# Hybrid decoder trunk on one core: the order of the last input tiles, the place of the scan's norm, and the order of the channels where the input projection turns into the output projection

## The reference

```python
h = rms_norm(x, norm_g)
u = h @ w_in
c_q, c_kv, k_pe, g_mla, u_conv, g_conv, z, xbc, dt_raw = jnp.split(u, offs, axis=-1)
o_mla = mla_mixer(...) * jax.nn.silu(g_mla)                  # 768 features
o_conv = conformer_conv_mixer(u_conv, ...) * jax.nn.silu(g_conv)   # 512; ends in layer_norm, silu, @ w_pw
o_ssd = ssd_mixer(z, xbc, dt_raw, ...)                       # 768; rms_norm(y * silu(z), norm_g)
y = jnp.concatenate([o_mla, o_conv, o_ssd], axis=-1) @ w_out
return x + y
```

## Time and profile before

| | |
|---|---|
| time, median of 3 runs | 1558.3 us (1558.18 to 1559.57) |
| profiled execution, its own time | 1560.33 us |
| its span in the trace | 1558.5 us |
| TensorE busy | 98% of the span |
| VectorE busy | 65% |
| ScalarE busy | 44% |
| mean DMA rate | 101 GB/s |

### The profile page before, as it was taken

The page is one execution under the profiler, slowest core; times in us unless marked ns, Lnnn a source line. Parts: engine busy times, 40 slices in busy tenths (PEclk is TensorE's granted clock), DMA queues, the critical chain, the costliest instruction groups (busy, mean ns, idle before and its releaser), DMA issues.

```text
span 1558.5 us, 18374 instructions
## 1 busy us (share of the span) xinstructions
PE 1525.9 (98%) x7062; PEld 1222.7 (78%) x7062; DVE 1007.0 (65%) x1496; ACT 687.6 (44%) x1014; POOL 44.7 (3%) x86
## 2 busy tenths in 40 slices
PE   7999999999999999999999999999999999999997
PEld 6777777778888887888887777778878887878885
DVE  7534674889998777443455456758999977762221
ACT  6445553434456645121253555533444575451110
POOL 0000000000000000110000000000000000000110
PEclk9999999999999999999999999999999999999999
DMA  6322222222233223544432222222223333234441
GB/s 224 94 92 81 82 82 81 68 82 68 81 111 114 89 83 96 176 142 142 142 102 78 87 89 82 95 68 68 77 73 102 99 116 98 88 99 158 150 140 62
DMA packets 44423, 158.13 MB, mean 101 GB/s; under 512 B 5520, under 2 KB 5808, under 8 KB 44336
## 3 DMA queue, kind: packets, MB, share of 16 engines
q1 hardware_dynamic: 36720, 129.64, 25.6%
q0 software_dynamic: 6464, 23.12, 5.1%
q10 hardware_dynamic: 1152, 4.19, 0.7%
HBM read 148.50 MB, written 8.44 MB: 101 GB/s over the span
## 4 chain that ended last, share of the span: by engine, by line
PE 84%; DVE 9%; ACT 4%; issue 1%; DMA 1%; ACTq 0%; DVEq 0%; POOL 0%; POOLq 0%
PE acc L494 19%; PE acc L496 18%; PE acc L495 18%; PE S L499 5%; PE S L494 3%; PE S L496 3%; PE S L495 3%; PE T L496 3%; PE T L494 3%; PE T L495 3%; DVE wlo L1022 2%; ACT L742 1%; PE M L499 1%; PE O L499 1%; DVE hlo L1105 1%
## 5 line engine op out<-in xcount | busy, mean ns | idle before, releaser
L494 PE MATMUL acc<-hhi,whi 128*128 128x512 f32 (+1 forms) x1504 | 600.6, 399 | 14.0 <-DVE wlo L1022 13.4
L496 PE MATMUL acc<-hhi,wlo 128*128 128x512 f32 (+1 forms) x1504 | 588.2, 391 | 0.0
L495 PE MATMUL acc<-hlo,whi 128*128 128x512 f32 (+1 forms) x1504 | 587.4, 391 | 0.0
L1022 DVE TENSOR_TENSOR wlo<-stage,whi 128x1024 fp32r<-128x1024 f32 (+2 forms) x252 | 300.7, 1196 | 411.5 <-ACT whi L754 408.1
L754 ACT ACTIVATE whi<-stage 128x1024 fp32r<-128x1024 f32 (+2 forms) x252 | 260.2, 1036 | 503.7 <-PE acc L496 281.4
L494 PEld LDWEIGHTS acc<-hhi,whi 128*128 128x128 f32 (+1 forms) x1504 | 282.2, 188 | 79.1 <-DVE wlo L1022 15.1
L496 PEld LDWEIGHTS acc<-hhi,wlo 128*128 128x128 f32 (+1 forms) x1504 | 281.8, 187 | 62.2
L495 PEld LDWEIGHTS acc<-hlo,whi 128*128 128x128 f32 (+1 forms) x1504 | 282.3, 188 | 60.8 <-issue 2.9
L1077 DVE SCALAR_TENSOR_TENSOR cacc<-glu,pv,cacc 128x512 f32<-128x512 f32 x240 | 168.8, 747 | 4.3 <-DVE cols L1161 0.3
L742 ACT ACT_TABLE_LOAD x67 | 86.0, 1283 | 7.5 <-issue 5.2
L494 PE MATMUL S<-hhi,whi 128*128 128x512 f32 x192 | 75.2, 392 | 0.0
(11 more groups left out here) (231 smaller groups left out, 1554.2 us busy)
## 6 DMA issues: line engine op xcount, KB each, us to landing
stage<-weights SPq DMA_DIRECT2D x236, 512.0 KB, 3.4
y_features<-xg POOLq DMA_DIRECT2D x32, 256.0 KB, 4.2
acsb<-acs_rows POOLq DMA_DIRECT2D x16, 384.0 KB, 4.1
xg<-x_features ACTq DMA_DIRECT2D x8, 512.0 KB, 9.3
xr<-x_features POOLq DMA_DIRECT2D x16, 256.0 KB, 4.1
xr<-y_features POOLq DMA_DIRECT2D x16, 256.0 KB, 4.1
stage<-weights SPq DMA_DIRECT2D x8, 256.0 KB, 2.6
stage<-weights SPq DMA_DIRECT2D x4, 384.0 KB, 3.0
```

Of the source, the lines that this page charges most:

```text
L494: nc.tensor.matmul(out, a, c, start=start, stop=False)
L495: nc.tensor.matmul(out, a, d, start=False, stop=False)
L496: return nc.tensor.matmul(out, b, c, start=False, stop=stop)
L1022: nc.vector.tensor_tensor(wlo[u % RING][:, 0:w], stage[u % STAGE][:, 0:w], whi[u % RING][:, 0:w].bitcast(F32), ALU.subtract).then_inc(lo_d ...
```

## The change

It does three things.

1. The last ten input tiles stand in the order z0, z1, z2, gconv0, gconv1, z3, z4, z5, gconv2, gconv3. z5 is now tile 38 (half tiles 76 and 77), gconv2 and gconv3 are tiles 39 and 40.
2. The scan's norm leaves the turn. `ssd_sum` is a hook of half tile 78, behind pw 0: TensorE waits for `ssd_sq` and multiplies by ones into bank `T[1]`, ScalarE does Ln and Exp. `ssd_scale` is a hook of half tile 79, behind pw 1: VectorE scales channels 10 to 15.
3. At the turn the channels are split and multiplied in the order `TURN_ORDER`: 0 to 7, then 10 to 15, then 8 and 9. The `out2` quarters take k = 0 to 7 for both rows first, then 10 to 15 for both, then 8 and 9. What was left of the old step `ssd_sum` is the step `turn_end`, which splits 10 to 15, then 8 and 9, and waits for the third and fourth pointwise product only ahead of 8 and 9.

```diff
-    t += [("gconv", j, [(_OFF["gconv"] + P * j, P)]) for j in range(4)]
-    t += [("z", j, [(_OFF["z"] + P * j, P)]) for j in range(6)]
-    return t
+    gate = [("gconv", j, [(_OFF["gconv"] + P * j, P)]) for j in range(4)]
+    z = [("z", j, [(_OFF["z"] + P * j, P)]) for j in range(6)]
+    return t + z[0:3] + gate[0:2] + z[3:6] + gate[2:4]
...
+    put(78, "ssd_sum")
+    put(79, "ssd_scale")
...
-    s.append(("ssd_sum", (), []))
+    s.append(("turn_end", (), []))
...
-OUT2 = [(0, k) for k in range(10)] + [(1, k) for k in range(10)]
-OUT2 += [(f, k) for f in range(2) for k in range(10, KX)]
+TURN_ORDER = list(range(8)) + list(range(10, KX)) + [8, 9]
+OUT2 = [(f, k) for f in range(2) for k in TURN_ORDER[:8]]
+OUT2 += [(f, k) for f in range(2) for k in TURN_ORDER[8:14]]
+OUT2 += [(f, k) for f in range(2) for k in TURN_ORDER[14:]]
...
+                    elif name == "ssd_sum":
+                        pe.wait_ge(ssd_sq.sem, ssd_sq.at(layer, 1))
+                        pe.wait_ge(ssd_in.sem, ssd_in.at(layer, 8))
+                        total(ssd_sum, [sqz[:, :]], T[1])
                     elif name == "out2":
...
-                        if quarter == 1:
-                            pe.wait_ge(ssd_sq.sem, ssd_sq.at(layer, 1))
-                            pe.wait_ge(pw_taken.sem, pw_taken.at(layer, 4))
-                            total(ssd_sum, [sqz[:, :]], M)
                         for i in range(8):
                             f, k = OUT2[8 * quarter + i]
-                            pe.wait_ge(h_lo.sem, h_lo.at(layer, KX + k + 1))
+                            pe.wait_ge(h_lo.sem, h_lo.at(layer, KX + TURN_ORDER.index(k) + 1))
...
                     elif name == "ssd_sum":
+                        act.wait_ge(ssd_sum.sem, ssd_sum.at(layer, 1))
+                        rsqrt(ssd_r, rcq[:, :], T[1][:, :], SSD_WIDTH, 0)
+                    elif name == "turn_end":
 
                         act.wait_ge(unit_used.sem, unit_used.at(layer, TILE_UNIT[len(TILES) - 1] + 1))
-                        act.wait_ge(pw_taken.sem, pw_taken.at(layer, 4))
-                        for k in range(8, KX):
-                            if k == 10:
-                                act.wait_ge(ssd_sum.sem, ssd_sum.at(layer, 1))
-                                rsqrt(ssd_r, rcq[:, :], M[:, :], SSD_WIDTH, 0)
+                        for k in TURN_ORDER[8:]:
                             if k >= 10:
                                 act.wait_ge(branch_ready.sem, branch_ready.at(layer, k - 9))
+                            else:
+                                act.wait_ge(pw_taken.sem, pw_taken.at(layer, k - 5))
                             branch_hi(k)
...
                     elif name == "turn":
-                        split_branch(0, 8)
-                    elif name == "ssd_sum":
-                        split_branch(8, 10)
+                        split_branch(TURN_ORDER[:8], 0)
+                    elif name == "ssd_scale":
                         dve.wait_ge(ssd_r.sem, ssd_r.at(layer, 1))
                         for k in range(10, KX):
                             stt(branch_ready, xg[:, k, :], xg[:, k, :], par("sng", k - 10), rcq[:, :], ALU.mult,
                                 ALU.mult, go=k < KX - 1)
-                            if k >= 12:
-                                split_branch(k - 2, k - 1)
-                        split_branch(KX - 2, KX)
+                    elif name == "turn_end":
+                        split_branch(TURN_ORDER[8:], 8)
```

More of the change, by code:

```diff
@@ L710, in _ @@
                             pe.wait_ge(acc_taken.sem, acc_taken.at(layer, len(TILES) - 1 + quarter))
-                        if quarter == 1:
-                            pe.wait_ge(ssd_sq.sem, ssd_sq.at(layer, 1))
-                            pe.wait_ge(pw_taken.sem, pw_taken.at(layer, 4))
-                            total(ssd_sum, [sqz[:, :]], M)
                         for i in range(8):
                             f, k = OUT2[8 * quarter + i]
-                            pe.wait_ge(h_lo.sem, h_lo.at(layer, KX + k + 1))
+                            pe.wait_ge(h_lo.sem, h_lo.at(layer, KX + TURN_ORDER.index(k) + 1))
                             last = three(out_bank(f)[:, :], *w(u, i * P, P), hhi[:, k, :], hlo[:, k, :],
-                                         k == 0, k == KX - 1)
+                                         k == 0, k == TURN_ORDER[-1])
                         last.then_inc(unit_used.sem, 1)
@@ L1099, in _, with split_branch @@
                         x_lo(k, 0)
-                def split_branch(first, end):
-                    for k in range(first, end):
-                        dve.wait_ge(h_hi.sem, h_hi.at(layer, KX + k + 1))
+                def split_branch(ks, before):
+                    for i, k in enumerate(ks):
+                        dve.wait_ge(h_hi.sem, h_hi.at(layer, KX + before + i + 1))
                         nc.vector.tensor_tensor(hlo[:, k, :], xg[:, k, :], hhi[:, k, :].bitcast(F32),
```

## The result

The changed kernel takes 1563.8 us (median of 12 runs, 1562.2 to 1565.1), the kernel before 1558.4 us (12 runs, 1558.0 to 1561.6). The ratio is 1.0027 with an interval of 1.0018 to 1.0035: slower by 0.27%, 4.2 us. The time lies in the range of the prediction, on the side of its rival B, and not at its point of 1559.8. The profiled execution took 1562.68 us around a span of 1560.9.

A forecast was written before the change was run, and what follows sets the result against it. TensorE, busy 98% of the span, bounds the kernel, so only its waits count. A layer loses 4.47 us at half tile 78 and regains 3.69 at the turn: +1.6 us in two, 1559.8 us from 1558.3; range 1557.0 to 1565.0.

The forecast's parts named there:

- rival B: In the stand at half tile 78 the clock falls: 2.4 us a fall, 1562.2 or 1564.6 us; chance 0.20.
- The wait at 78: Behind half tile 78 and pw0 TensorE waits for z5's last add; half tile 79 comes 4.47 us later.
- The turn: Both TensorE waits at the turn go: 3.69 us a layer back, 0.87 us of it only the ones-matmul moved.
- Rival D: At the turn waits of the old size stay, the scaling having delayed the eight splits: 1565.4 us; chance 0.08.
- The sum without the clock: A layer: +4.47 us at half tile 78 less 3.69 us at the turn, +0.78 us.
- the hitch inside quarter 2: A 0.1 us loss inside quarter 2 of `out2` at the turn, named only as an allowance in the range.
- The tiles, ScalarE and the scaling: Half tiles 62 to 67, norm table loads and 4.1 us of scaling passes stay hidden, costing the path nothing.
- A: TensorE's wait moves from the turn to half tile 78: 1559.8 us, called same; chance 0.64.
- The price of a fall: Behind the stand at half tile 78, twelve matmuls at 0.2 us more each: 2.4 us a fall.
- Rival C: At half tile 78 TensorE stands under 1.6 us, so the turn's gain decides: 1551.7 us, faster; chance 0.08.

The follow-up runs named there:

- e5: The changed kernel with one number changed: the hook `ssd_sum` at half tile 79 in place of 78, the scaling still at 79; 1553.7 us, ratio 0.9966.
- e7: The changed kernel with `ln_apply` 1 at half tile 77 in place of 76, behind z5's passes on VectorE; 1564.4 us, ratio 1.0031.
- e1: The changed kernel with four extra ones-matmuls, result overwritten, in TensorE's stand at half tile 78; 1562.15 us, ratio 1.0009.
- e11: The changed kernel with the attention stand filled and four extra ones-matmuls in the stand at half tile 78; 1559.2 us, ratio 0.9998.
- e8: The kernel before with two extra ones-matmuls ahead of the first transposition of probabilities, in attention; 1558.24 us, ratio 0.9994.
- e6: The changed kernel with one extra ones-matmul, result overwritten, in the stand at half tile 78; 1562.4 us, ratio 1.0018.
- e10: The changed kernel with the attention stand filled by extra ones-matmuls, nothing added at half tile 78; 1562.6 us, ratio 1.0018.
- e4: The kernel before with one wait added: behind half tile 78 and pw0 TensorE waits for z3's last add; 1570.9 us, ratio 1.0065.

## Why the prediction was right and where not

**The wait at 78** was right in place, cause and size: behind pw0, for the last add of z5, in VectorE's order behind `ln_apply`. TensorE stood 3.7 us by the profile's count, and the norm's matmul started 0.05 us behind the end of the add, not 0.15. e5 and e7 show the cause: one half tile later there is no stand, and with VectorE's order turned the stand moves to pw0.

**The turn** gave back what was forecast. No wait is left there; the scaling ends at 598.83, 1.8 us before the eight splits begin; the last quarter's weights are split in time. Rival D is out.

**The sum without the clock** was +0.78 us a layer and measured +0.53 (e1, e11). The term is over by 0.25 us: 0.1 is the shorter way from the add to the matmul, about 0.1 the hitch inside quarter 2 that also went, which I had named and not counted; the rest isn't resolved.

**The tiles, ScalarE and the scaling** cost nothing, as forecast. VectorE's idle time ahead of the split of half tile 68 shrank from 2.72 us to 0.67 us, by three passes, and the split itself, at 511.28 with the 1.89 us added, starts at the old 513.17:

```profile
511.28 1.23 DVE L1027 TENSOR_TENSOR wlo<-stage,whi 128x1024 fp32r<-128x1024 f32 x1 [0.67 <-ACT whi L758]
```

The additional table load for gconv2 is there at 589.59, under pw1 (588.66 to 591.47 on TensorE).

**The step that failed is the weight between A and B.** The likeliest case was a stand that costs its length, 1559.8 us, called the same; what happened is B, the fall in both layers, which had 0.20. The prediction said that the trace couldn't decide, since the spacing stayed 0.23 us behind the longest stands of the turn. That read too few rows. The windows of the granted clock in the kernel before show a fall at 240 to 246, behind a stand of 1.56 us, less than half as long as the one forecast. The like stand of layer 1 had none, so the trace made a fall possible and not certain; but a stand over twice as long should have had more than 0.20. The price of a fall was over: 2.4 us forecast, as twelve matmuls at half rate from the start of the kernel, 1.6 measured (55.92 less 54.30). The half clock lasted only 3.4 us here, and about 1.0 us of the price lay in the norm's own matmul and the product behind it, the rest in the next four. B's own sum, 1564.6, is high by 0.8 us of the median, the two errors of size going one way (-0.25 and -0.8 a layer), and the falls in attention, which come on top in most runs, the other. That it came so near is in part luck.

**Rival C** is out: there was no short wait.

In time without falls the change would cost 1.0 us (e11 against e8: runs of 1558.8 to 1559.7 against 1557.9 to 1558.9), under the 3.1 us that the prediction needed to tell a change from none. The measured 4.2 us are those 1.0 and two falls of 1.6. The stand itself was no small matter: e5, which has neither stand nor fall at 78, is 5.1 us a layer under the changed kernel, 3.5 more than the fall.

## What to carry to other kernels

When a join is moved earlier on TensorE, look up when its last input is made in the order of the engine that makes it; one half tile was the difference between 0.27% lost and 0.34% won. Where TensorE must stand between dense matmuls, count the fall of the clock behind the stand as well as the stand: here 1.6 us for most, 2.6 to 2.9 for some, behind stands of 1.6 to 4.3 us. Matmuls with a discarded result took the fall away where they filled nearly the whole stand (four in e1 and e11, 0.3 us of stand left); one of them was not enough (e6, 2.9 us left). And read the windows of the granted clock of the kernel before, since a fall that is already there warns of what a new stand may do.

## What the runs showed of the hardware

The clock fell behind a stand of only 1.56 us in some executions of the same program (e8 against the kernel before), and in one layer of the profiled execution and not the other. It fell at a stand of 2.9 us in both layers of the profiled execution (e6), at stands of 3.7 and 4.3 us in every layer profiled, and not behind the waits of the turn, of 1.4 us at most.

Where it fell relative to the stand differs. In the changed kernel and e6 it was 0.1 to 0.3 us behind the end of the stand, in attention 1.1 to 1.8 us behind it, in the second layer of e10 1.4 us behind it. In e4, e7 and the first layer of e10 it was inside the stand, by 0.5 to 1.3 us; so the spacing of matmuls does not show all of it.

The half clock lasted 3.4 us in twelve of the fifteen falls that the profiles here show, and 6.8 us in three: both layers of e4 and the first of e10. The price follows from that: of 3.4 us at half rate about half is lost, 1.7 us by this estimate against 1.6 measured. Of the 6.8 us a part (0.6, 1.3 and 1.0 us) lay in the stand, where it costs nothing, and half of the rest makes 3.1, 2.8 and 2.9 us against 2.9, 2.6 and 2.8 measured. Why the same stand of 3.7 us brought the short fall in some layers and the long one in others is open. In all three long ones the clock fell over half a microsecond before the stand ended, but e7 has falls that began nearly as early and stayed short.

The Trainium skill, "TensorE: Matmul & The Clock Gate", Part 1 on the clock gate, says that idleness throttles the array and sustained work frees it. The trace agrees in kind: 0.43 us between matmuls behind the stand, and 0.23 again further on, with TensorE at work throughout.
